# Six slots instead of four through one token tile and then the other around the post-normed sums, and two chunks of the wide layer by rows

## The chip, the cores and the metric

The kernel runs on one core of a Trainium2 chip. Its time is the device time of one execution in microseconds (us). Five engines work side by side and wait for each other through semaphores: PE (TensorE, matmuls), DVE (VectorE), ACT (ScalarE), POOL (GpSimd) and SP, which here only issues the transfers of the weights. Each engine takes its own list of instructions strictly in the order in which it is written: an instruction whose semaphore isn't there yet holds up all that stand behind it on its engine.

## The reference

The program is a small network on 256 tokens of 1024 channels: a state-space layer and an attention layer, and then two blocks of this form (cut to what the change touches):

```
h = rms_norm(x, ln_mix_pre)
merged = g0 * y_mla + g1 * y_conv + g2 * y_ret          # three branches of h, gated
x = x + rms_norm(merged @ w_out, ln_mix_post)           # a post-normed sum
h = rms_norm(x, ln_ffn_pre)
f = (silu(h @ w_gate) * (h @ w_up)) @ w_down            # hidden width 2816
x = x + rms_norm(f, ln_ffn_post)                        # the other post-normed sum
```

All is float32. Each of the two blocks has two post-normed sums, four in all. After three of them the next layer follows (the second norm of block 0, the first norm of block 1, the second norm of block 1); the fourth ends the program.

## The kernel before

**Slots.** The weights are streamed in the order of their use, as slots of 2 x 128 input rows by 512 columns (512 KB; 416 columns in the chunk called lat). A chunk is 512 columns of a weight matrix: `out.` has two chunks of 4 slots, the wide layer `ffn.` 11 chunks of 4 slots (256 gate and 256 up columns side by side), `down.` two chunks of 11 slots. There are six buffers for slots. SP loads a slot as soon as PE is through with the slot six places before it (`sp.wait_ge(slot_used, before[s] + 1)`). To keep float32's precision every operand is split in a high and a low part: ACT writes the high part of a slot's weights (`make_hi`, L1146), DVE the low part (`make_lo`, L1611), and PE multiplies hi x hi, lo x hi and hi x lo (L629 to L631): 6 matmuls of 512 columns for each slot and tile of 128 tokens. I call these six matmuls a tile-slot.

**Order on PE.** `run(n)` takes n slots one after the other, both token tiles of each. `by_tile(n, ...)` takes n slots for token tile 0 and then the same n slots for token tile 1, with steps that are put in before a given tile and slot: `go` transposes four blocks of the next layer's input, `have` waits for their high and low parts. In this way the norm of tile 0 can be worked out while PE is still on tile 1. Buffers of a `by_tile` group come free only in its second half. Chunks of `ffn.` other than the first are computed the other way round (`hidden_slot`, L606 to L608: weights stationary, 12 x 2 matmuls of 256 columns), which gives the hidden layer with its channels on the partitions, as `down.` needs it; the first chunk is computed by rows, since its input isn't there for both tiles at once, and is transposed afterwards (`L{l}.f0`, L1059).

**Order on ACT and DVE.** It is written by hand. `splits(n)` makes the high (ACT) or low (DVE) parts of all slots below n that aren't made yet. `evac` reads a chunk's sums: for `out.` and `down.` ACT squares and adds them (L1180) and DVE multiplies them by the gain into `h_T` (L1644). `post_normed_tail` orders the work behind a post-normed sum for tile 0 and tile 1: `evac`, root on POOL (`root_of_sums`, L2422 and L2407), `residual` (DVE, `x_T`, L1641), `norm_square` (ACT, L1180), a second root on POOL, `apply_norm` (DVE, `h_T`, L1641), the transposes on PE (L684), `tile_hi` (ACT, L1197) and `tile_lo` (DVE, L1641), with `splits` in between.

## Time and profile before

| | us |
|---|---|
| median of 3 runs | 1307.27 (1306.84 to 1309.51) |
| the profiled execution | 1308.64 |
| its span | 1306.8 |
| PE busy | 1248.0 (95%) |
| DVE busy | 920.1 (70%) |
| ACT busy | 633.7 (48%) |
| PE waiting for DVE's `h_T` before the transposes of L684 | 3.7 in 5 waits |
| PE waiting for DVE's `act_F_lo` (L1641) before L629 | 6.5 in 5 waits |

The span is the time between the first and the last record of the profiled execution; some 2 us of its time lie outside. PE is the busy engine nearly everywhere, so time is what PE needs plus what PE waits. Matmuls overlap in the records, so the pace of PE is read from the distance of their starts, not from their durations.

### The profile page before, as it was taken

The numbers are of one execution on the slowest core, as the hardware profiler recorded it, in microseconds if no ns is written. First come the engines' busy times: TensorE is split into PE (matmuls) and PEld (weight loads), VectorE is DVE, ScalarE is ACT, GpSimd is POOL, SyncE is SP. The second block draws the span as 40 slices with busy tenths as digits, with TensorE's granted clock in tenths as the row PEclk, the third lists the DMA queues.
The fourth block names the chain that finished last, engine by engine and source line by source line (L and its number), as shares of the span: only waits on it lengthen the run. The fifth ranks groups of instructions, "written<-read, shape, count | busy, mean of one in ns | idle before, by whom it ended". The sixth has DMA issues, their size and how long they took to land.

```text
span 1306.8 us, 18772 instructions
## 1 busy us (share of the span) xinstructions
PE 1248.0 (95%) x7461; PEld 1039.6 (80%) x7461; DVE 920.1 (70%) x1501; ACT 633.7 (48%) x977; POOL 113.3 (9%) x189
## 2 busy tenths in 40 slices
PE   7799899898999999999999999999999999999998
PEld 3466678787878878777899987888878777999986
DVE  7797778566578997686665554678997686665553
ACT  4334465454555555544544444555555535544442
POOL 7600012000100100201000001100100201000000
PEclk9989999899999999999999999999999999999999
DMA  6734556442664544355656565564444354555553
GB/s 239 210 89 141 181 187 191 130 129 87 193 207 151 157 145 146 121 171 161 193 178 185 186 184 174 186 203 160 146 148 147 125 168 170 167 188 179 183 189 112
DMA packets 71958, 215.73 MB, mean 165 GB/s; under 512 B 16256, under 2 KB 19744, under 8 KB 71744
## 3 DMA queue, kind: packets, MB, share of 16 engines
q1 hardware_dynamic: 65008, 206.43, 49.9%
q0 software_dynamic: 2112, 6.97, 1.7%
q10 hardware_dynamic: 4752, 1.14, 0.4%
q8 instruction: 59, 0.97, 0.3%
q14 instruction: 27, 0.22, 0.1%
HBM read 209.01 MB, written 3.15 MB: 162 GB/s over the span
## 4 chain that ended last, share of the span: by engine, by line
PE 74%; DVE 13%; POOL 4%; ACT 4%; DMA 2%; issue 2%; ACTq 0%; DVEq 0%; POOLq 0%
PE acc L629 16%; PE acc L631 15%; PE acc L630 15%; PE acc L607 6%; PE acc L608 6%; PE acc L606 6%; DVE weights_lo L1611 4%; DVE conv_acc_F L1641 2%; DMA weights_raw<-stream_dram 2%; PE mixed L937 1%; PE acc L569 1%; PE mixed L947 1%; ACT weights_hi L1146 1%; PE mixed L1016 1%; POOL stat L2407 1%
## 5 line engine op out<-in xcount | busy, mean ns | idle before, releaser
L1611 DVE TENSOR_TENSOR weights_lo<-weights_raw,weights_hi 128x1024 fp32r<-128x1024 f32 (+2 forms) x364 | 442.6, 1231 | 230.5 <-ACT weights_hi L1146 229.4
L1146 ACT ACTIVATE weights_hi<-weights_raw 128x1024 fp32r<-128x1024 f32 (+2 forms) x364 | 375.9, 1046 | 293.6 <-DMA weights_raw<-stream_dram 293.4
L629 PE MATMUL acc<-weights_hi,act_F_hi 128*128 128x512 f32 (+1 forms) x896 | 365.0, 407 | 14.0 <-DVE act_F_lo L1641 6.5
L631 PE MATMUL acc<-weights_hi,act_F_lo 128*128 128x512 f32 (+1 forms) x896 | 354.6, 396 | 0.0
L630 PE MATMUL acc<-weights_lo,act_F_hi 128*128 128x512 f32 (+1 forms) x896 | 354.5, 396 | 0.0
L629 PEld LDWEIGHTS acc<-weights_hi,act_F_hi 128*128 128x128 f32 x896 | 170.3, 190 | 54.9 <-DVE act_F_lo L1641 8.0
L631 PEld LDWEIGHTS acc<-weights_hi,act_F_lo 128*128 128x128 f32 x896 | 170.1, 190 | 38.6
L630 PEld LDWEIGHTS acc<-weights_lo,act_F_hi 128*128 128x128 f32 x896 | 170.3, 190 | 35.1
L608 PE MATMUL acc<-act_F_lo,weights_hi 128*128 128x256 f32 x640 | 182.5, 285 | 0.0
L607 PE MATMUL acc<-act_F_hi,weights_lo 128*128 128x256 f32 x640 | 181.9, 284 | 0.0
L606 PE MATMUL acc<-act_F_hi,weights_hi 128*128 128x256 f32 x640 | 180.4, 282 | 0.0
L606 PEld LDWEIGHTS acc<-act_F_hi,weights_hi 128*128 128x128 f32 x640 | 121.8, 190 | 0.1
L608 PEld LDWEIGHTS acc<-act_F_lo,weights_hi 128*128 128x128 f32 x640 | 121.2, 189 | 0.0
L607 PEld LDWEIGHTS acc<-act_F_hi,weights_lo 128*128 128x128 f32 x640 | 120.6, 188 | 0.1
L1641 DVE SCALAR_TENSOR_TENSOR conv_acc_F<-conv_in_F,conv_params,conv_acc_F 128x256 f32<-128x256 f32 x240 | 98.0, 481 | 0.0
L631 PE MATMUL acc<-weights_hi,ffn_F_lo 128*128 128x512 f32 x176 | 69.6, 395 | 0.0
L630 PE MATMUL acc<-weights_lo,ffn_F_hi 128*128 128x512 f32 x176 | 69.6, 395 | 0.0
L629 PE MATMUL acc<-weights_hi,ffn_F_hi 128*128 128x512 f32 x176 | 69.6, 395 | 0.0
L2422 POOL TENSOR_SCALAR stat<-stat 128x1 f32<-128x1 f32 x18 | 9.3, 518 | 638.5 <-ACT junk L1180 638.5
L569 PE MATMUL acc<-weights_raw,hn_F 128*128 128x512 f32 x128 | 58.9, 609 | 0.0
L569 PEld LDWEIGHTS acc<-weights_raw,hn_F 128*128 128x128 f32 x128 | 24.5, 200 | 26.1 <-issue 26.1
L630 PEld LDWEIGHTS acc<-weights_lo,ffn_F_hi 128*128 128x128 f32 x176 | 33.1, 188 | 8.0
(309 smaller groups left out, 1332.4 us busy)
## 6 DMA issues: line engine op xcount, KB each, us to landing
weights_raw<-stream_dram SPq DMA_DIRECT2D x364, 512.0 KB, 3.5
gains<-rows_dram POOLq DMA_DIRECT2D x12, 512.0 KB, 4.8
weights_raw<-stream_dram SPq DMA_DIRECT2D x8, 416.0 KB, 3.2
weights_raw<-stream_dram SPq DMA_DIRECT2D x4, 384.0 KB, 3.0
x_T<-x_in_dram SPq DMA_DIRECT2D x4, 256.0 KB, 6.1
ssm_bc<-ssm_bc_dram SPq DMA_DIRECT2D x1, 1024.0 KB, 8.6
u_scratch<-u_T ACTq DMA_DIRECT2D x4, 256.0 KB, 3.8
u_sub<-u_scratch SPq DMA_DIRECT2D x4, 256.0 KB, 2.8
```

Source lines behind the costliest of these rows:

```text
L569: i = pe.matmul(acc[par][t][:, 0:w], f0[:, k, t * P:(t + 1) * P], raw[:, place[pos], kk * w:(kk + 1) * w], start=first and kk == 0, stop=l ...
L606: pe.matmul(o, wh, hi[:, k, :], start=first and kk == 0 and m % 2 == 0, stop=False, skip_group_check=True)
L607: pe.matmul(o, wl, hi[:, k, :], start=False, stop=False, skip_group_check=True)
L608: i = pe.matmul(o, wh, lo[:, k, :], start=False, stop=last and kk == s["nk"] - 1, skip_group_check=True)
L629: pe.matmul(o, xh, wh, start=first and kk == 0, stop=False)
L630: pe.matmul(o, xh, wl, start=False, stop=False)
L631: i = pe.matmul(o, xl, wh, start=False, stop=last and kk == s["nk"] - 1)
L937: x = pe.matmul(b[:, qt * SEQ:(qt + 1) * SEQ], qk[0:dk, i % 2, qt * P:(qt + 1) * P], qk[0:dk, i % 2, SEQ:2 * SEQ], start=True, stop=True)
L947: x = pe.matmul(b[:, qt * dv:(qt + 1) * dv], probs_t[:, h % 2, qt, kt, :], src_v(kt, h), start=(kt == 0), stop=(kt == TT - 1))
L1146: act.activation(w_hi[:, place[s], 0:n], raw[:, place[s], 0:n], ACT.Copy).then_inc(hi_made, 1)
L1611: dve.tensor_tensor(low(s, slice(0, n)), raw[:, place[s], 0:n], w_hi[:, place[s], 0:n].bitcast(F32), ALU.subtract).then_inc(lo_made, 1)
L1641: return dve.scalar_tensor_tensor(out=o, in0=a, scalar=s, in1=b, op0=op0, op1=op1)
```

## The change

On PE, in each block: the eight slots of `out.` were taken as 2 x `by_tile(4)`, now as `by_tile(2)` and `by_tile(6)`; the first `by_tile(4)` of the wide layer becomes `by_tile(6)` (all of its first chunk and half of the second); the last four slots of `down.` and the four of the next block's `lat.` become groups of six too (in block 1 the last four slots of `down.` stay). The transposes of tile 0's normed input stand before the last slot of tile 1 (`(1, DEEP - 1)`), not behind it. The second chunk of the wide layer is computed by rows and transposed like the first. ACT's and DVE's orders are rewritten for this.

```diff
-FFN_F = HT // 2 - 1
+FFN_T = 2
+FFN_F = HT // 2 - FFN_T
+DEEP = 6
...
             for l in range(DEPTH2):
-                by_tile(4, {(0, 0): [go(0, 0), go(0, 1), have(0, 0)] if l else [have(0, 0)], (0, 2): [have(0, 1)],
-                            (0, 3): [go(1, 0), go(1, 1)], (1, 0): [have(1, 0)], (1, 2): [have(1, 1)]})
-                run(7)
+                n = DEEP if l else 4
+                by_tile(n, {(0, 0): [have(0, 0)], (0, 2): [have(0, 1)],
+                            (0, n - 1): [go(1, 0), go(1, 1)], (1, 0): [have(1, 0)], (1, 2): [have(1, 1)]})
+                run(11 - n)
...
-                by_tile(4, {(0, 0): [have(0, 0)], (0, 2): [have(0, 1), go(1, 1)], (1, 0): [have(1, 0)], (1, 2): [have(1, 1)]})
-                by_tile(4, {})
-                go, have = norm_turner(f"L{l}.h2", 3 + 2 * l)
-                by_tile(4, {(0, 0): [go(0, 0), go(0, 1), have(0, 0)], (0, 2): [have(0, 1)],
-                            (0, 3): [go(1, 0), go(1, 1)], (1, 0): [have(1, 0)], (1, 2): [have(1, 1)]})
-                run(4)
-                pe.wait_ge(ffn0_hid, TT * (l + 1))
-                b = mix(f"L{l}.f0", hid_lo, HT // 2 * l + 1)
+                by_tile(2, {(0, 0): [have(0, 0), have(1, 0), go(1, 1)]})
+                go2, have2 = norm_turner(f"L{l}.h2", 3 + 2 * l)
+                by_tile(DEEP, {(0, 0): [have(0, 1)], (1, 0): [have(1, 1)], (1, DEEP - 1): [go2(0, 0), go2(0, 1)]})
+                by_tile(DEEP, {(0, 0): [have2(0, 0)], (0, 2): [have2(0, 1)],
+                               (0, DEEP - 1): [go2(1, 0), go2(1, 1)], (1, 0): [have2(1, 0)], (1, 2): [have2(1, 1)]})
+                run(4 * FFN_T - DEEP + 3)
+                pe.wait_ge(ffn0_hid, TT * FFN_T * (l + 1))
+                for c in range(FFN_T):
+                    b = mix(f"L{l}.f{c}", hid_lo, HT // 2 * l + c + 1)
...
-                run(HT // 2 - 4)
-                by_tile(4, {})
                 if l + 1 < DEPTH2:
                     go, have = norm_turner(f"L{l + 1}.h", 4 + 2 * l)
+                    run(HT // 2 - DEEP)
+                    by_tile(DEEP, {(1, DEEP - 1): [go(0, 0), go(0, 1)]})
+                else:
+                    run(HT // 2 - 4)
+                    by_tile(4, {})
...
 # ACT, post_normed_tail
-                splits(end + 1)
-                evac(f"L{l}.{kind}1", [0])
-                splits(end + 2)
+                splits(end)
+                for chunk in last:
+                    evac(chunk, [0])
...
-                evac(f"L{l}.{kind}1", [1])
+                splits(end + 1)
                 for half in range(2):
                     tile_hi(name, 0, half, ahead=2)
+                for chunk in last:
+                    evac(chunk, [1])
                 splits(end + 3)
                 for half in range(2):
                     norm_square(name, 1, half, x_normed, x_at + half + 3)
+                splits(end + 5)
                 for half in range(2):
-                    tile_hi(name, 1, half, ahead=4)
+                    tile_hi(name, 1, half, ahead=1)
```

The instructions themselves hardly change; what changes is their order. Three places are shown, in block 0.

On PE, where the gated branches are summed (`gates_T`) and `out.` begins; before the change (rows left out are matmuls of the same kind):

```order
L630 MATMUL acc<-weights_lo,conv_F_hi 128x512
L631 MATMUL acc<-weights_hi,conv_F_lo 128x512
L629 MATMUL acc<-weights_hi,act_F_hi 128x512 [waits conv_weighed,weights_lo_made,turned_lo_made]
L630 MATMUL acc<-weights_lo,act_F_hi 128x512
L631 MATMUL acc<-weights_hi,act_F_lo 128x512
...
L684 MATMUL turned<-consts,gates_T 128x128 [waits merged,turned_lo_made]
L684 MATMUL turned<-consts,gates_T 128x128 x3
```

The same place after the change:

```order
L637 MATMUL acc<-weights_lo,conv_F_hi 128x512
L638 MATMUL acc<-weights_hi,conv_F_lo 128x512
L691 MATMUL turned<-consts,gates_T 128x128 [waits turned_lo_made,merged]
L691 MATMUL turned<-consts,gates_T 128x128 x3
L636 MATMUL acc<-weights_hi,act_F_hi 128x512 [waits conv_weighed,weights_lo_made]
L637 MATMUL acc<-weights_lo,act_F_hi 128x512
```

The last transposes of the summed branches (tile 1, second half) have moved from behind two tile-slots of `out.` to directly behind the matmuls whose sums they need.

On ACT, behind the first post-normed sum (`junk,stat<-acc` is a square of the sums, `junk,stat<-x_T` one of the residual, `weights_hi` a split, `act_F_hi` is `tile_hi`), before the change, from the square of tile 0's last chunk on:

```order
L1180 ACTIVATE junk,stat<-acc 128x512 [waits post_sums,first_tiles_done]
L1146 ACTIVATE weights_hi<-weights_raw 128x1024 [waits weights_in1]
L1180 ACTIVATE junk,stat<-x_T 128x512 [waits post_sums,x_normed]
L1180 ACTIVATE junk,stat<-x_T 128x512 [waits norm_sums,x_normed]
L1180 ACTIVATE junk,stat<-acc 128x512 [waits norm_sums,slots_used]
L1197 ACTIVATE act_F_hi<-turned 128x4x128 [waits turned_ready] x2
L1146 ACTIVATE weights_hi<-weights_raw 128x1024 [waits weights_in2]
...
L1146 ACTIVATE weights_hi<-weights_raw 128x1024 [waits weights_in3]
```

After the change, from the split of the wide layer's first slot (`weights_in0`) on:

```order
L1158 ACTIVATE weights_hi<-weights_raw 128x1024 [waits weights_in0]
L1209 ACTIVATE act_F_hi<-turned 128x4x128 [waits turned_ready] x2
L1192 ACTIVATE junk,stat<-acc 128x512 [waits norm_sums,slots_used]
L1192 ACTIVATE junk,stat<-acc 128x512 [waits post_sums,slots_used]
L1158 ACTIVATE weights_hi<-weights_raw 128x1024 [waits weights_in1]
L1158 ACTIVATE weights_hi<-weights_raw 128x1024 [waits weights_in2]
L1192 ACTIVATE junk,stat<-x_T 128x512 [waits post_sums,x_normed]
L1192 ACTIVATE junk,stat<-x_T 128x512 [waits norm_sums,x_normed]
L1158 ACTIVATE weights_hi<-weights_raw 128x1024 [waits weights_in3]
L1158 ACTIVATE weights_hi<-weights_raw 128x1024 [waits weights_in4]
L1209 ACTIVATE act_F_hi<-turned 128x4x128 [waits turned_ready] x2
L1158 ACTIVATE weights_hi<-weights_raw 128x1024 [waits weights_in5]
```

The splits of the second and later slots of the next group now stand behind the squares of tile 1 (`slots_used`); before, the first two were done ahead of them.

On DVE at the same place (`h_T<-acc,gains` is `evac`, `x_T` the residual, `h_T<-x_T` the norm, `act_F_lo` is `tile_lo`, `weights_lo` a split), before the change, from tile 0's norm on:

```order
L1641 SCALAR_TENSOR_TENSOR h_T<-x_T,stat,gains 128x512
L1611 TENSOR_TENSOR weights_lo<-weights_raw,weights_hi 128x1024 [waits weights_hi_made]
L1644 TENSOR_TENSOR h_T<-acc,gains 128x512 [waits gain_in0,post_sums,slots_used]
L1641 SCALAR_TENSOR_TENSOR act_F_lo<-turned,act_F_hi 128x4x128 [waits turned_hi_made]
L1641 SCALAR_TENSOR_TENSOR x_T<-h_T,stat,x_T 128x512 [waits post_roots,mix_scaled]
```

After the change, likewise:

```order
L1656 SCALAR_TENSOR_TENSOR h_T<-x_T,stat,gains 128x512
L1626 TENSOR_TENSOR weights_lo<-weights_raw,weights_hi 128x1024 [waits weights_hi_made]
L1656 SCALAR_TENSOR_TENSOR act_F_lo<-turned,act_F_hi 128x4x128 [waits turned_hi_made] x2
L1659 TENSOR_TENSOR h_T<-acc,gains 128x512 [waits gain_in0,post_sums,slots_used] x2
L1626 TENSOR_TENSOR weights_lo<-weights_raw,weights_hi 128x1024 [waits weights_hi_made] x2
L1656 SCALAR_TENSOR_TENSOR x_T<-h_T,stat,x_T 128x512 [waits post_roots,mix_scaled]
L1656 SCALAR_TENSOR_TENSOR x_T<-h_T,stat,x_T 128x512
L1626 TENSOR_TENSOR weights_lo<-weights_raw,weights_hi 128x1024 [waits weights_hi_made]
```

Both low parts of tile 0 now stand ahead of tile 1's `evac`; of the six slots of the next group one is split ahead of it, two behind it, and one behind the residual (then come the norm of tile 1, one more split, `tile_lo` twice, and the sixth split).

## Rows read from the trace of the kernel before

**Rows 1.** The page's first part: busy us (share of the span), instructions.

```profile
PE 1248.0 (95%) x7461; PEld 1039.6 (80%) x7461; DVE 920.1 (70%) x1501; ACT 633.7 (48%) x977; POOL 113.3 (9%) x189
```

**Rows 2.** Waits of PE over the span: us in total, times, longest.

```profile
PE acc L629 <- DVE act_F_lo L1641: 6.5, 5, 1.6
...
PE acc L629 <- DVE weights_lo L1611: 3.4, 8, 1.4
```

**Rows 3.** Timeline of PE, begin of block 0's `out.`: start, us, instruction.

```profile
594.47 0.39 PE L629 MATMUL acc<-weights_hi,act_F_hi 128*128 128x512 f32 x1
...
597.25 0.60 PE L684 MATMUL turned<-consts,gates_T 128*128 128x128 f32 x4
597.60 0.48 PE L629 MATMUL acc<-weights_hi,act_F_hi 128*128 128x512 f32 x1
```

**Rows 4.** Timeline of PE, end of block 0's `out.` and on.

```profile
617.73 0.40 PE L631 MATMUL acc<-weights_hi,act_F_lo 128*128 128x512 f32 x1
618.86 1.29 PE L684 MATMUL turned<-consts,h_T 128*128 128x128 f32 x8 [0.74 <-DVE h_T L1641]
621.77 0.50 PE L629 MATMUL acc<-weights_hi,act_F_hi 128*128 128x512 f32 x1 [1.61 <-DVE act_F_lo L1641]
...
623.61 0.63 PE L629 MATMUL acc<-weights_hi,act_F_hi 128*128 128x512 f32 x1
624.04 0.63 PE L630 MATMUL acc<-weights_lo,act_F_hi 128*128 128x512 f32 x1
...
635.46 0.28 PE L606 MATMUL acc<-act_F_hi,weights_hi 128*128 128x256 f32 x1
...
646.86 0.60 PE L1059 MATMUL mixed<-consts,ffn_hid_F 128*128 128x128 f32 x4
```

**Rows 5.** Timeline of PE, end of block 0's `down.` and the next block's `lat.`.

```profile
812.35 0.40 PE L631 MATMUL acc<-weights_hi,ffn_F_lo 128*128 128x512 f32 x1
...
816.80 0.35 PE L629 MATMUL acc<-weights_hi,act_F_hi 128*128 128x416 f32 x1
816.99 0.35 PE L630 MATMUL acc<-weights_lo,act_F_hi 128*128 128x416 f32 x1
...
827.67 0.40 PE L629 MATMUL acc<-weights_hi,act_F_hi 128*128 128x512 f32 x1
```

**Rows 6.** Timeline of PE, block 1: begin of `out.` and end of `ffn.0`.

```profile
1083.34 0.39 PE L629 MATMUL acc<-weights_hi,act_F_hi 128*128 128x512 f32 x1
...
1123.77 0.28 PE L606 MATMUL acc<-act_F_hi,weights_hi 128*128 128x256 f32 x1
```

**Rows 7.** Timeline of ACT, end of block 0's `out.`.

```profile
612.58 0.60 ACT L1180 ACTIVATE junk<-acc 128x512 f32<-128x512 f32 x1 [0.72 <-PE acc L631]
...
613.17 1.05 ACT L1146 ACTIVATE weights_hi<-weights_raw 128x1024 fp32r<-128x1024 f32 x1
...
618.16 0.60 ACT L1180 ACTIVATE junk<-acc 128x512 f32<-128x512 f32 x1 [1.38 <-PE acc L631]
...
619.53 1.26 ACT L1197 ACTIVATE act_F_hi<-turned 128x512 fp32r<-128x512 f32 x2 [0.68 <-PE turned L684]
```

**Rows 8.** Timeline of DVE, end of block 0's `out.`.

```profile
613.36 0.69 DVE L1644 TENSOR_TENSOR h_T<-acc,gains 128x512 f32<-128x512 f32 x1 [0.20 <-issue]
...
614.46 1.41 DVE L1641 SCALAR_TENSOR_TENSOR x_T<-h_T,stat,x_T 128x512 f32<-128x512 f32 x2 [0.40 <-POOL stat L2407]
...
617.97 1.42 DVE L1641 SCALAR_TENSOR_TENSOR h_T<-x_T,stat,gains 128x512 f32<-128x512 f32 x2 [2.10 <-POOL stat L2407]
...
619.30 1.22 DVE L1611 TENSOR_TENSOR weights_lo<-weights_raw,weights_hi 128x1024 fp32r<-128x1024 f32 x1
```

**Rows 9.** Timeline of POOL, end of block 0's `out.`.

```profile
616.88 0.30 POOL L2422 TENSOR_SCALAR stat<-stat 128x1 f32<-128x1 f32 x1 [2.54 <-ACT junk L1180]
...
618.95 1.66 POOL L2422 TENSOR_SCALAR stat<-stat 128x1 f32<-128x1 f32 x1 [1.11 <-ACT junk L1180]
```

**Rows 10.** Source view of the slots' loads (L1127), 590 to 640 us.

```profile
DMA to landing us min/median/max: 3.2/4.7/5.4
```

**Rows 11.** Timeline of DVE, begin of block 0's `out.`: the last sum of the gated branches.

```profile
595.47 0.69 DVE L1644 TENSOR_TENSOR gates_T<-gates_T 128x512 f32<-128x512 f32 x1
```

117 lines of the change are left out of this document (64 added, 53 removed).

## The prediction

> **What bounds the kernel now.** I read the page's busy shares first, then the waits of PE, and then the timeline of PE, ACT, DVE and POOL around the post-normed sums, each at the same stretch. PE is busy 95% of the span, DVE 70% [rows 1], and of its waits those for `act_F_lo` and for `weights_lo` matter here [rows 2]. So the time is PE's work at the full clock (2.4 GHz) plus what PE waits, and a change of order can only move waits. The reader is to see three things.
>
> First, PE's pace. Twelve matmuls of 512 columns start between 594.47 and 597.25, where the transposes come [rows 3]: 0.232 us each, 1.39 us for a tile-slot of six. A slot of the wide layer in the other form takes (646.86 - 635.46) / 4 = 2.85 us [rows 4] against 2.78 for two tile-slots. A tile-slot of lat has starts 0.19 apart [rows 5]: 1.14.
>
> Second, what a post-normed sum costs now. PE is through with tile 1 of `out.` at 617.96 (617.73 and one pace) and starts the wide layer at 621.77; between them lie 0.8 us of transposes and 3.0 of waiting. From 621.77 to 635.46 it does 48 matmuls and eight transposes, 11.9 us of work, in 13.7: starts stand 0.43 apart for a while, not 0.23 [rows 4], the lower clock level of 1.2 GHz behind a stretch of waiting. The loss is 4.8 us (3.0 and 1.8). Block 1 does the same work from the start of `out.` on in 40.4 us, block 0 in 41.0 [rows 3, 4, 6], so I take the same loss there. At the end of `down.`, from 812.58 to 827.67, PE does 8 tile-slots of lat and 16 transposes (10.7) in 15.1, a loss of 4.4 [rows 5]. The three together are 14.0 us: all that the change can take away.
>
> Third, the chain of tile 0 behind its last matmul: from the square at 612.58 to the transposes at 618.86 it is 6.3 us, over DVE, POOL, DVE, ACT, POOL, DVE [rows 4, 7 to 9]. Tile 1 of four slots covers 5.56 us, tile 1 of six covers 8.34.
>
> **The change, part by part.** I reckon from T, the moment when PE is through with the last tile-slot before the norm, and number the slots of `out.` 0 to 7, those of the next layer 8 to 13.
>
> *Tile 0's chain is covered.* With the transposes before the last slot, PE reaches them 5 x 1.39 = 6.95 us after tile 0's end; the first half of the norm is there after 6.5, the second 0.7 later, and the four transposes of the first half lie between. `tile_hi` follows 0.67 after its transposes and `tile_lo` 0.6 later [rows 4, 7], within the last slot's 1.39. The 3.0 us of waiting are gone at each place. What is late next is the weights.
>
> *The new group's weights.* All six buffers belong to the group that PE is working on, and the next group's slots can be split only as tile 1 frees them. The order lets one of the six be split before tile 1's sums, the rest behind. From T, with the durations of the rows:
> - Slot 8 is ready, PE works on it until T+1.4. ACT's square of tile 1 starts at T+0.2 (617.96 to 618.16), the high part of slot 9 takes T+0.8 to T+1.85 [rows 7]; DVE's `evac` starts 0.78 behind the square and lasts 0.6, the low part takes 1.22 [rows 8]: done at T+3.1. PE waits **1.8**.
> - DVE splits slot 10 (T+4.3) and then does the residual, whose first half is there at T+4.9; only then come ACT's two squares (T+5.0, 0.8 apart), and behind them the high part of slot 11 (T+6.4 to T+7.5) and its low part (to T+8.75). PE wanted it at T+5.95: **2.8**.
> - DVE does tile 1's norm from T+8.65 (the root on POOL is there at T+7.6, one microsecond behind the sums [rows 9]) to T+10.0, then the low part of slot 12 to T+11.2. PE wanted it at T+10.15: **1.1**.
> - After slot 12 PE transposes tile 1 (T+12.6 to T+13.4). Slot 13 is split behind both `tile_hi` and both `tile_lo`: T+13.3, two of them 1.0, the high part to T+15.35, the low part from T+15.4 to T+16.6. PE wanted it at T+13.4: **3.2**.
>
> The sum is 8.9 us. Slot loads take 3.2 to 5.4 us from issue to landing [rows 10]; slots 9 to 12 were freed between T-6.4 and T-2.2 and slot 13 at T, and would have landed before the point at which the order reaches them, so the transfers are not what PE waits for here. The last slot of a six-group is freed only five tile-slots (6.95) before its use: 0.3 + 4.7 + 1.05 + 1.2 = 7.25, another **0.3** in `out.`.
>
> *The merge.* PE passes the last transposes of `gates_T` directly behind the matmuls of which they are made. At 594.47 PE goes on to `out.` today; DVE's last sum ends at 596.16 [rows 3, 11]. PE will wait **1.75** us there, twice, and everything on PE is behind it. Today 12 matmuls cover it.
>
> *Sum for `out.`,* from PE's start on it to the end of slot 13: 1.75 + 0.35 (four transposes) + 16 tile-slots of 22.25 + 0.8 + 0.3 = 25.4 to T; then 16.6, a tile-slot of 1.4, and tile 1 of six, 8.3: 51.8 us. Today the same slots take 635.46 - 594.47 + 2 x 2.85 = 46.7 in block 0 and 1123.77 - 1083.34 + 5.7 = 46.1 in block 1 [rows 3, 4, 6]. **+5.1 and +5.7.**
>
> *Sum for `down.`:* the same steps with lat's shorter tile-slots and splits (832 columns for 1024) give waits of 1.7, 2.8, 1.3 and 3.2; slot 13 begins at T+15.75. From the start of the six slots (812.58 - 16.7 = 795.9) it is 16.7 + 0.8 + 15.75 + 1.4 + 4 x 1.14 + 2.8 = 42.0; today to 827.67 and two slots of 2.78 more, 37.3 [rows 5]. **+4.6.**
>
> *The second chunk by rows.* Two more slots in the cheaper form per block, -0.15; four more transposes with the restart behind them, 0.35 + 0.1; two `ffn_F_lo` now stand on DVE ahead of the next weight split, some 0.2. Per block +0.5, in all **+1.0**; its bounds are -0.3 (hidden altogether) and +2.
>
> *The clock.* No row shows PE with this pattern of waits. Below, it is nothing: a half-speed matmul that lies in front of a wait costs nothing, since DVE sets the pace there. Above, two stretches at the lower level per place, 1.8 us each by the loss found above. I take one per place, like two of today's three: 3 x 1.8 = **+5.4**, and keep 0 and 10.8 as ends. The Trainium skill (TensorE: Matmul & The Clock Gate, section "HAM oscillation — how this bites in real kernels") says that short work between long waits falls back to the low clock again and again, and reckons the penalty as half of the time spent there; by that rule it would be the upper end, 5 us more than my sum. This trace agrees in so far as the starts of rows 4 are 0.43 apart after a wait, and disagrees at `down.`, where the starts stay 0.19 apart.
>
> POOL's first operation of a root took 0.30 us once and 1.66 when DVE was splitting weights beside it [rows 8, 9]. With more splits beside the roots tile 1's norm can come up to 0.4 us later at each place; I leave that in the range. The Trainium skill (SBUF — State Buffer, section "Who interferes with whom") has the rule behind it: the two engines share a pair of ports that one holds for a whole instruction.
>
> Total: 5.1 + 5.7 + 4.6 + 1.0 + 5.4 = **+21.8 us**. The profiled execution took 1308.64 us (span 1306.8 and some 2 us outside); it becomes 1330.4. It stands 1.4 above the median of the runs, 1307.27, so I forecast 1329.
>
> **The rivals.**
> *The cover works and nothing takes its place (faster).* The mechanism is the ring of six buffers: it decides whether slots 9 to 13 are split by the time PE wants them. If they were, as slots 8 to 11 are today, PE would get back 4.8 + 4.8 + 4.4 and pay 2 x 1.75 at the merge and 1.0 for the chunk: -9.5, 1298. The point is 1.39 us behind T: slot 9's low part there or not. For it speaks that DVE is idle 30% of the time; against it that ACT has the split written behind a square that can't start before T. 6 in 100.
> *No change.* The waits of one or two of the six steps are half of mine (shorter handovers, `evac` earlier) and the clock stays up: this needs 15 us of error in a chain whose terms are read one by one. 2 in 100. With part of that, a time of 1310 to 1319: 7 in 100.
> *The clock falls twice and more at each place.* 16.4 + 10.8 and the late roots: +28, 1335 or above. The broken work in the 15 us behind T speaks for it, only five of them are PE's; against it `down.` today. 12 in 100.
> *Transfers.* Six slots in one go could land ever later. At 1.39 us between frees they landed after 4.7, at most 5.4 [rows 10]; each us beyond 5.4 would add at most 1 at slot 9 and nothing at the others. Inside my range.
>
> **How the numbers follow.** Forecast as worked out (1320 to 1335): 73 in 100, the others as above. Slower in all is 92, faster 6, no change 2 (within 0.2%, 2.6 us, about what a measurement of this kernel can tell). The range leaves the faster case and the smallest of the slower ones out and goes from 1316 to 1338.
>
> **What would show it.** In the timeline of PE after the change: the transposes of `h_T` without a wait before them; four waits for `weights_lo` in the first half of each six-slot group, before its second, fourth, fifth and sixth slot, the last the longest (3 us); a wait of 1.7 before the last transposes of `gates_T`, twice. PE's waits for `weights_lo` should sum to 25 to 30 us (3.4 today over the whole kernel [rows 2]), those for `act_F_lo` shrink. ACT's split of slot 9 should start within a microsecond behind the square of tile 1. If PE doesn't wait for `weights_lo` there, the prediction is wrong in its main step; if the waits are there but the sum of time is smaller, the clock term is.

## The result, and the profile after

| | before | after |
|---|---|---|
| median of 4 runs each, us | 1307.05 (1304.73 to 1309.51) | 1333.23 (1331.00 to 1334.67) |
| ratio, 95% interval | | 1.0209 (1.0183 to 1.0235) |
| profiled execution, span | 1308.64, 1306.8 | 1331.00, 1328.8 |
| granted clock over the span | 0.990 | 0.986 (the four runs: 0.983 to 0.986) |

The change makes the kernel 2.1% slower, 26 us. I forecast 1329 with a range of 1316 to 1338. The spans of the two profiled executions differ by 22.0 us; the medians by 4 more, since the profiled execution of the kernel after is the fastest of its four and that of the kernel before lies 1.6 us above its median.

The page's first part, of the kernel after (it answers to [rows 1]):

```profile
PE 1249.8 (94%) x7373; PEld 1034.8 (78%) x7373; DVE 920.2 (69%) x1505; ACT 632.9 (48%) x979; POOL 110.0 (8%) x189
```

PE has 1.8 us more busy time, DVE and ACT have the same to within 1 us: what the change adds is waiting. PE's waits over the span, of the kernel after (us in total, times, longest; [rows 2] before):

```profile
PE acc L636 <- DVE weights_lo L1626: 27.8, 18, 2.9
...
PE turned L691 <- DVE gates_T L1659: 4.0, 4, 1.7
...
PE turned L691 <- DVE h_T L1656: 1.5, 2, 1.2
PE acc L636 <- DVE act_F_lo L1656: 1.5, 1, 1.5
```

The waits for split weights went from 3.4 to 27.8 us; those for `act_F_lo` fell from 6.5 to 1.5, and those for `h_T` from 3.7 to 1.5 (the rest lies elsewhere). Tile 0's chain is covered, as the change wants, and another wait has taken its place. Where it stands shows the timeline of PE in block 0, of the kernel after:

```profile
592.55 0.40 PE L638 MATMUL acc<-weights_hi,conv_F_lo 128*128 128x512 f32 x1
594.63 0.63 PE L691 MATMUL turned<-consts,gates_T 128*128 128x128 f32 x4 [1.68 <-DVE gates_T L1659]
...
616.25 1.03 PE L691 MATMUL turned<-consts,h_T 128*128 128x128 f32 x8
...
618.29 0.39 PE L638 MATMUL acc<-weights_hi,act_F_lo 128*128 128x512 f32 x1
...
621.66 0.50 PE L636 MATMUL acc<-weights_hi,act_F_hi 128*128 128x512 f32 x1 [1.58 <-DVE weights_lo L1626]
...
627.24 0.50 PE L636 MATMUL acc<-weights_hi,act_F_hi 128*128 128x512 f32 x1 [2.51 <-DVE weights_lo L1626]
...
629.70 0.50 PE L636 MATMUL acc<-weights_hi,act_F_hi 128*128 128x512 f32 x1 [0.79 <-DVE weights_lo L1626]
...
635.19 0.50 PE L636 MATMUL acc<-weights_hi,act_F_hi 128*128 128x512 f32 x1 [2.94 <-DVE weights_lo L1626]
...
636.09 0.63 PE L636 MATMUL acc<-weights_hi,act_F_hi 128*128 128x512 f32 x1
636.51 0.63 PE L637 MATMUL acc<-weights_lo,act_F_hi 128*128 128x512 f32 x1
...
652.19 0.28 PE L613 MATMUL acc<-act_F_hi,weights_hi 128*128 128x256 f32 x1
```

The eight transposes at 616.25 have no wait (they had 0.74, and 1.61 behind them [rows 4]). The last matmul of `out.` starts at 618.29, so PE is through with it at 618.52, one pace later. The four waits behind are the second, fourth, fifth and sixth slot of the wide layer. From 636.09 the starts stand 0.43 apart, the lower clock level. Who made PE wait is seen on ACT and DVE, first ACT, of the kernel after, same stretch:

```profile
618.72 0.60 ACT L1192 ACTIVATE junk<-acc 128x512 f32<-128x512 f32 x1 [0.17 <-PE acc L638]
...
623.44 0.63 ACT L1192 ACTIVATE junk<-x_T 128x512 f32<-128x512 f32 x1 [2.15 <-DVE x_T L1656]
...
624.89 1.99 ACT L1158 ACTIVATE weights_hi<-weights_raw 128x1024 fp32r<-128x1024 f32 x2
631.85 1.08 ACT L1209 ACTIVATE act_F_hi<-turned 128x512 fp32r<-128x512 f32 x2 [4.97 <-PE turned L691]
632.82 1.06 ACT L1158 ACTIVATE weights_hi<-weights_raw 128x1024 fp32r<-128x1024 f32 x1
```

And DVE, of the kernel after:

```profile
622.66 1.41 DVE L1656 SCALAR_TENSOR_TENSOR x_T<-h_T,stat,x_T 128x512 f32<-128x512 f32 x2
625.96 1.23 DVE L1626 TENSOR_TENSOR weights_lo<-weights_raw,weights_hi 128x1024 fp32r<-128x1024 f32 x1 [1.89 <-ACT weights_hi L1158]
...
632.48 1.29 DVE L1656 SCALAR_TENSOR_TENSOR act_F_lo<-turned,act_F_hi 128x512 fp32r<-128x512 f32 x2 [2.83 <-ACT act_F_hi L1209]
633.91 1.22 DVE L1626 TENSOR_TENSOR weights_lo<-weights_raw,weights_hi 128x1024 fp32r<-128x1024 f32 x1
```

PE, ACT and DVE wait for each other in turn. ACT stands idle for 2.15 us in front of the residual's squares (623.44) although the fourth slot's split is written behind them, and DVE then idles 1.89 for that split (625.96). Both idle (4.97 and 2.83 us) in front of tile 1's parts, although the sixth slot's split stands behind them. No row of the stretch ends on a transfer.

In block 1's `out.` the waits are 1.61, 2.54, none and 2.94. At `down.` and lat the same four waits as in block 0 appear (1.48, 2.47, 0.98 and 2.89), and two things more. PE, of the kernel after, from the fifth slot on:

```profile
828.29 0.79 PE L636 MATMUL acc<-weights_hi,act_F_hi 128*128 128x512 f32 x1 [0.98 <-DVE weights_lo L1626]
831.01 1.91 PE L691 MATMUL turned<-consts,h_T 128*128 128x128 f32 x8
835.81 0.80 PE L636 MATMUL acc<-weights_hi,act_F_hi 128*128 128x512 f32 x1 [2.89 <-DVE weights_lo L1626]
...
854.96 0.50 PE L636 MATMUL acc<-weights_hi,act_F_hi 128*128 128x512 f32 x1 [2.38 <-DVE weights_lo L1626]
```

First, the clock. A view of stretches, of the kernel after (from 827.2 to 840.9 us; us, then busy time and count of PE, PEld, DVE, ACT, POOL; granted clock, share of the transfers, GB/s):

```profile
827.20:840.90 13.70, 9.83 (x29) 7.95 (x29) 3.78 (x6) 2.14 (x3) 0.53 (x1) 0.51 0.25 81
```

13.7 us at a granted clock of 0.51, that is the lower of the two levels (1.2 GHz); the slot and the eight transposes from 828.29 on take twice their time (1.91 us for the transposes against 1.03 at 616.25). Second, a wait of 2.38 us 19 us later, which the kernel before doesn't have. On ACT, of the kernel after:

```profile
844.29 1.06 ACT L1158 ACTIVATE weights_hi<-weights_raw 128x1024 fp32r<-128x1024 f32 x1 [9.79 <-DMA weights_raw<-stream_dram]
846.82 1.06 ACT L1158 ACTIVATE weights_hi<-weights_raw 128x1024 fp32r<-128x1024 f32 x1 [1.47 <-DMA weights_raw<-stream_dram]
847.79 0.50 ACT L1243 ACTIVATE lat_T<-acc 128x416 f32<-128x416 f32 x1
```

The reading of lat's sums, and the norm behind them (on DVE at 852.37, after 3.23 us of waiting for POOL's root), stand behind the splits of two slots whose transfers could start only when the group's second half freed their buffers.

**The sum.** Milestones on PE, from the timelines of the two kernels (`out.` counted from the end of conv_o.; "slot 15" is the end of the wide layer's second chunk). The rows not yet shown, first of the kernel before:

```profile
750.98 0.40 PE L629 MATMUL acc<-weights_hi,ffn_F_hi 128*128 128x512 f32 x1
847.19 0.27 PE L724 MATMUL turned<-consts,lat_norm_T 128*128 128x128 f32 x1
1135.16 0.27 PE L1059 MATMUL mixed<-consts,ffn_hid_F 128*128 128x128 f32 x1
1239.29 0.40 PE L629 MATMUL acc<-weights_hi,ffn_F_hi 128*128 128x512 f32 x1
```

Then of the kernel after:

```profile
755.82 0.39 PE L636 MATMUL acc<-weights_hi,ffn_F_hi 128*128 128x512 f32 x1
817.79 0.40 PE L638 MATMUL acc<-weights_hi,ffn_F_lo 128*128 128x512 f32 x1
843.86 0.35 PE L638 MATMUL acc<-weights_hi,act_F_lo 128*128 128x416 f32 x1
863.44 0.27 PE L731 MATMUL turned<-consts,lat_norm_T 128*128 128x128 f32 x1
1101.48 0.63 PE L691 MATMUL turned<-consts,gates_T 128*128 128x128 f32 x4 [1.68 <-DVE gates_T L1659]
1157.94 0.28 PE L613 MATMUL acc<-act_F_hi,weights_hi 128*128 128x256 f32 x1
1261.56 0.39 PE L636 MATMUL acc<-weights_hi,ffn_F_hi 128*128 128x512 f32 x1
```

| stretch | before | after | difference | forecast |
|---|---|---|---|---|
| start to `out.`, block 0 (same code) | 594.47 | 592.78 | -1.7 | 0 |
| `out.` to slot 15 | 52.39 | 59.41 | +7.0 | 5.1 + 1.8 |
| wide layer to `down.` | 104.12 | 103.63 | -0.5 | +0.5 |
| `down.` to sixth slot of block 1 | 82.2 | 91.0 | +8.8 | 4.6 + 1.8 |
| to the transposes of lat | 14.0 | 16.6 | +2.6 | 0 |
| to `out.`, block 1 | 236.15 | 236.2 | 0 | 0 |
| `out.` to slot 15 | 51.82 | 58.3 | +6.5 | 5.7 + 1.8 |
| wide layer to `down.` | 104.13 | 103.62 | -0.5 | +0.5 |
| `down.` to the end | 67.5 | 67.2 | -0.3 | 0 |
| sum | 1306.8 | 1328.8 | +22.0 | +21.8 |

(592.78 is 592.55 and one pace; 1099.63, the end of conv_o. in block 1, is the transposes' 1101.48 less block 0's distance of 1.85; the sixth slot ends two tile-slots of 1.39 behind 843.86 + 0.19, and before the change two slots of 2.78 behind 827.67. The -0.5 of the wide layer, twice, is a difference in the pace of its matmuls and not what the second chunk costs; see x_rows below.)

### The profile page after: what moved, and what is told of

Same layout as the page of the kernel before. It is cut to its first block, busy times and chain, and to the rows that moved or that the text cites. A ratio compares the mean times of both kernels' runs of the same rounds, so it can differ in the third digit from the quotient of the medians.

```text
span 1328.8 us, 18602 instructions
## 1 busy us (share of the span) xinstructions
PE 1249.8 (94%) x7373; PEld 1034.8 (78%) x7373; DVE 920.2 (69%) x1505; ACT 632.9 (48%) x979; POOL 110.0 (8%) x189
## 4 chain that ended last, share of the span: by engine, by line
PE 72%; DVE 14%; ACT 5%; POOL 4%; DMA 2%; issue 2%; ACTq 0%; DVEq 0%; POOLq 0%
PE acc L636 15%; PE acc L638 15%; PE acc L637 15%; PE acc L613 5%; PE acc L615 5%; PE acc L614 5%; DVE weights_lo L1626 5%; DVE conv_acc_F L1656 2%; DMA weights_raw<-stream_dram 2%; ACT weights_hi L1158 2%; PE mixed L944 1%; PE acc L576 1%; PE mixed L954 1%; POOL stat L2434 1%; PE mixed L1024 1%
## 5 line engine op out<-in xcount | busy, mean ns | idle before, releaser
L636 PE MATMUL acc<-weights_hi,act_F_hi 128*128 128x512 f32 (+1 forms) x928 | 379.5, 409 | 33.0 <-DVE weights_lo L1626 27.8
L638 PE MATMUL acc<-weights_hi,act_F_lo 128*128 128x512 f32 (+1 forms) x928 | 368.2, 397 | 0.0
L637 PE MATMUL acc<-weights_lo,act_F_hi 128*128 128x512 f32 (+1 forms) x928 | 367.9, 396 | 0.0
L613 PE MATMUL acc<-act_F_hi,weights_hi 128*128 128x256 f32 x576 | 162.6, 282 | 0.0
L615 PE MATMUL acc<-act_F_lo,weights_hi 128*128 128x256 f32 x576 | 162.2, 282 | 0.0
L614 PE MATMUL acc<-act_F_hi,weights_lo 128*128 128x256 f32 x576 | 162.1, 281 | 0.0
L613 PEld LDWEIGHTS acc<-act_F_hi,weights_hi 128*128 128x128 f32 x576 | 108.4, 188 | 0.2
L614 PEld LDWEIGHTS acc<-act_F_hi,weights_lo 128*128 128x128 f32 x576 | 108.5, 188 | 0.1
L615 PEld LDWEIGHTS acc<-act_F_lo,weights_hi 128*128 128x128 f32 x576 | 108.4, 188 | 0.0
L1209 ACT ACTIVATE act_F_hi<-turned 128x512 fp32r<-128x512 f32 x32 | 18.4, 596 | 46.5 <-PE turned L691 46.3
```

Of the source, the lines that this page charges most:

```text
L613: pe.matmul(o, wh, hi[:, k, :], start=first and kk == 0 and m % 2 == 0, stop=False, skip_group_check=True)
L614: pe.matmul(o, wl, hi[:, k, :], start=False, stop=False, skip_group_check=True)
L615: i = pe.matmul(o, wh, lo[:, k, :], start=False, stop=last and kk == s["nk"] - 1, skip_group_check=True)
L636: pe.matmul(o, xh, wh, start=first and kk == 0, stop=False)
L637: pe.matmul(o, xh, wl, start=False, stop=False)
L638: i = pe.matmul(o, xl, wh, start=False, stop=last and kk == s["nk"] - 1)
```

## The experiments

All ratios are to the kernel before, run beside each kernel on the same chip; "us" is the median. The kernel before has medians of 1305.2 to 1307.1 us in the different experiments, so a difference between kernels of two experiments carries that much uncertainty beside the intervals. Below "second slot" and so on are slots of the new group, T the end of the group before, on PE.

| kernel | base and edit | us | ratio (95%) | clock, mean |
|---|---|---|---|---|
| x_last | after, sixth slot split ahead of tile 1's parts | 1320.5 | 1.0101 (1.0087 to 1.0115) | 0.989 |
| x_merge | after, transposes of `gates_T` later | 1325.1 | 1.0145 (1.0124 to 1.0167) | 0.987 |
| v_merge | before, transposes of `gates_T` early | 1310.7 | 1.0038 (1.0024 to 1.0052) | 0.991 |
| x_rows | before, second chunk by rows | 1305.1 | 0.9993 (0.9984 to 1.0003) | 0.992 |
| x_down | before, groups of six at `down.` only | 1314.3 | 1.0062 (1.0047 to 1.0076) | 0.990 |
| y_nine | x_last, second slot ahead of tile 1's squares | 1318.9 | 1.0089 (1.0060 to 1.0117) | 0.988 |
| y_eleven | x_last, fourth slot ahead of the residual's squares | 1316.7 | 1.0081 (1.0053 to 1.0108) | 0.990 |
| y_six | all four orders | 1311.2 | 1.0038 (1.0023 to 1.0053) | 0.991 |
| y_five | the same, groups of five | 1307.5 | 1.0007 (0.9994 to 1.0020) | 0.994 |
| w_six | y_six, `evac` and lat earlier | 1306.7 | 1.0002 (0.9991 to 1.0014) | 0.991 |
| w_five | y_five, the same, and `out.` as 2, 1, 5 | 1304.8 | 0.9986 (0.9977 to 0.9996) | 0.994 |
| v_pool | w_five, three low parts on POOL | 1308.1 | 1.0011 (0.9998 to 1.0024) | 0.990 (0.994 without one run at 0.944) |

(The before kernel's runs have a mean granted clock of 0.992, those of the kernel after 0.984.)

### x_last: the sixth slot ahead of tile 1's parts

```diff
 # ACT, and the same on DVE before tile_lo
-                splits(end + 5)
+                splits(end + 6)
                 for half in range(2):
                     tile_hi(name, 1, half, ahead=1)
```

> The kernel after, with the sixth slot's high and low parts written ahead of tile 1's `tile_hi` and `tile_lo` (ACT and DVE: `splits(end + 6)` for `splits(end + 5)`). Theory of the order: the 2.9 us that PE waits before the sixth slot at each of three places come only from the split standing behind both parts of tile 1; DVE stands idle for 4.5 us in front of them. The wait goes, and about 0.7 us comes back as a wait for `act_F_lo` one tile-slot later: 3 x -2.2 = -6.6 us, 1326 to 1328. Rival, the ring: the sixth slot's buffer is freed last, its weights have not landed any earlier and the wait stays at 2.5 us or more: 0 to -1 us.

Measured: 1320.5, about 13 us less than the kernel after (expected: 1326 to 1328). The wait is gone at all three places, and no other comes in its place. On DVE, of x_last, block 0, the last two low parts now stand together and it idles afterwards:

```profile
629.02 2.35 DVE L1626 TENSOR_TENSOR weights_lo<-weights_raw,weights_hi 128x1024 fp32r<-128x1024 f32 x2
634.74 0.69 DVE L1656 SCALAR_TENSOR_TENSOR act_F_lo<-turned,act_F_hi 128x512 fp32r<-128x512 f32 x1 [3.36 <-ACT act_F_hi L1209]
```

The theory of the order stands, the ring's doesn't: ACT makes three high parts in a row from 625.48 on (2.94 us, no wait for a transfer among them), the sixth slot's among them, so the buffer freed last was filled by 627.4, about 3 us before PE began the fifth slot (630.29). The gain is twice what I expected. The 0.7 us that should have come back did not (tile 1's parts are made while PE is on the sixth slot), which makes 3 x 2.9 = 8.8; the spans differ by 9.7. The rest of the medians' difference goes with the clock, 0.989 for 0.984.

### x_merge and v_merge: the merge, undone and done alone

```diff
 # x_merge, on the kernel after
-                by_tile(2, {(0, 0): [have(0, 0), have(1, 0), go(1, 1)]})
+                by_tile(2, {(0, 0): [have(0, 0)], (1, 0): [have(1, 0), go(1, 1)]})
 # v_merge, on the kernel before
-                by_tile(4, {(0, 0): [have(0, 0)], (0, 2): [have(0, 1), go(1, 1)], (1, 0): [have(1, 0)], (1, 2): [have(1, 1)]})
+                by_tile(4, {(0, 0): [have(0, 0), have(1, 0), go(1, 1)], (0, 2): [have(0, 1)], (1, 2): [have(1, 1)]})
```

> The kernel after, with the last transposes of `gates_T` behind two tile-slots of `out.`, as before the change. Theory of the merge: the waits of 1.68 us go at both places and nothing takes their place, since tile 1's second half is first wanted six tile-slots later: -3.4 us, about 1329.8. Rival: the start of `out.` only moves to an earlier time and PE meets the same chain of splits a little later; the waits for split weights before the second to sixth slot of the wide layer stand at a fixed distance from the end of `out.`, so this would need a wait inside `out.`; then 0 to -1 us.

> The kernel before with one edit: the last transposes of `gates_T` stand directly behind the matmuls whose sums they need, as in the change; everything else is as before. Prices the merge term from the other side: my prediction has 1.75 us at two places, +3.5. Undoing the same edit in the kernel after (x_merge) gave back 8 us in the medians. If that surplus belongs to the clock, which falls more often where several waits lie within 30 us, then here, with only one other wait of 2.4 us near, it stays at +3 to +4.5: 1309.5 to 1311, granted clock unchanged at 0.99. If the two waits themselves cost more than their length, it is +7 or more here too.

Measured: x_merge is 8 us faster than the kernel after, v_merge 5.0 us slower than the kernel before (interval 3.1 to 6.8). In both traces the wait of 1.68 us stands or goes at both places, with nothing in its place. v_merge is between its two cases, nearer to the first, and its interval holds the 3.4 us of the two waits themselves. In the kernel after, undoing the merge gave back 8 us in the medians; with both intervals that is some 4 to 13, and the spans of the profiled executions differ by 5.8. That the merge costs more there than alone is likely but not shown. If so, the surplus goes with the clock: in x_merge's profiled execution no stretch at `down.` is at the lower level as long as the 13.7 us above. That the waits themselves call the lower level up isn't shown.

### x_rows: the second chunk alone

```diff
 # kernel before; the wide layer's code as in the change, DEEP left at four
-FFN_F = HT // 2 - 1
+FFN_T = 2
+FFN_F = HT // 2 - FFN_T
```

> The kernel before, with only the second chunk of the wide layer by rows (groups of four slots everywhere). My prediction's term for it: +1.0 us in all (bounds -0.3 and +2). The trace of the kernel after, from the end of slot 15 to the start of `down.`, has 0.5 us less per block, not more: then -1.0 us against the kernel before. Rival: two chunks wanted at once from ACT and DVE hold up the splits behind them, +3 us or more.

Measured: 0.9993, -0.9 us, between -2.1 and +0.4, close to the -1.0 read from the kernel after. The forecast's +1.0 lies outside; no wait appears behind the two chunks. But the traces show that the -1.0 in the spans isn't what the chunk costs. The 256-column matmuls of a block start either 0.1199 or 0.1187 us apart, on the mean of some 860 of them, and that alone makes 1.0 to 1.2 us per block. In the profiled kernel before both blocks have the slower pace, in the profiled kernel after both the faster. v_merge has the kernel before's code there and the faster pace in block 0:

```profile
648.83 0.60 PE L1059 MATMUL mixed<-consts,ffn_hid_F 128*128 128x128 f32 x4
...
751.80 0.39 PE L629 MATMUL acc<-weights_hi,ffn_F_hi 128*128 128x512 f32 x1
```

| wide layer to `down.`, us | pace 0.1199 | pace 0.1187 |
|---|---|---|
| one chunk by rows | 104.1 (4 blocks: both of before, block 1 of x_down and v_merge) | 103.0 (block 0 of x_down and v_merge) |
| two chunks by rows | 104.6 (2 blocks: of x_merge and w_five) | 103.5 to 103.6 (the other 20 blocks) |

At the same pace the second chunk costs 0.4 to 0.7 us per block, as forecast. Why a block has one pace or the other, and whether it is chance that the slower one stands in four of six blocks of the old form and in two of 22 of the new, the runs don't show.

### x_down: groups of six at one place

```diff
 # kernel before; n = DEEP if l else 4 at the start of a block, six last slots of down. by tile,
 # and the change's ACT and DVE order for this place alone
+                (tail_of_six if kind == "down." and name else tail_of_four)(name, l, kind, no)
```

> The kernel before, with groups of six only at the end of block 0's `down.` and the start of block 1's `lat.`, one place of three. If the places are independent: the forecast's terms for it are 4.6 + 1.8 = +6.4 us; the trace of the kernel after has +11.4 there (8.8 in the groups, 2.6 in a wait behind `lat.`). I expect +9 to +12, with the wait of 2.4 us behind `lat.` there too. Rival: the wait behind `lat.` and the long stretch at the lower clock come from the kernel's other changes and not from this place; then +6 or less.

Measured: +8.1 us (6.1 to 9.9), less than the 9 to 12 that I expected. Waits of 1.49, 2.47, 1.05 and 2.94 in the group and of 1.84 behind lat stand in its trace. The place does by itself what it does in the whole change, a little less: its stretch at the lower level is shorter (820.5 to 829.9) and its wait behind lat too. The time alone would hardly exclude the rival's +6; the rows do, since both the wait and the stretch are there without the other changes.

### y_nine and y_eleven: which waits only move

```diff
 # y_nine, on x_last; the same on DVE
+                splits(end + 2)
                 for chunk in last:
                     evac(chunk, [1])
 # y_eleven, on x_last, ACT alone
-                splits(end + 3)
+                splits(end + 4)
                 for half in range(2):
                     norm_square(name, 1, half, x_normed, x_at + half + 3)
```

> The kernel x_last with the second slot of the new group split ahead of tile 1's squares (ACT) and of tile 1's `evac` (DVE). The prediction priced the wait before that slot as a term of its own. If the waits add up, the 1.5 us before the second slot go at three places: -4.5 us against x_last, 1316. Rival theory, DVE's list: behind T DVE has the same splits, residual and norm to do, in whatever order, so the 1.2 us come back before the fourth slot (its wait grows from 2.5 to over 3) and the time stays within 1 us of x_last's 1320.5; I hold this for likelier, since the square of tile 1, and with it the residual, now waits for that split.

> The kernel x_last with the fourth slot's high part ahead of the two squares of tile 1's residual on ACT (`splits(end + 4)` for `splits(end + 3)`), DVE as it is. In the trace of the kernel after ACT stands idle 1.9 us before those squares, and DVE 1.7 us before the fourth slot's low part. Theory of the order: the wait before the fourth slot falls from 2.5 to about 0.9 us, and the norm of tile 1 comes 0.5 us earlier: 3 x -1.6 to -2 = -5 to -6 us, 1315. Rival, the transfer: the slot has landed only a little before ACT reaches it, so it can't be split earlier: within 1 us of 1320.5.

Measured: y_nine 1318.9 (1.6 below x_last), y_eleven 1316.7 (3.8 below, for 5 to 6 expected). By the intervals of the ratios neither time differs from x_last's for certain; the waits in the rows decide. PE of y_nine, block 0:

```profile
623.24 0.47 PE L636 MATMUL acc<-weights_hi,act_F_hi 128*128 128x512 f32 x1 [0.76 <-DVE weights_lo L1627]
627.59 0.50 PE L636 MATMUL acc<-weights_hi,act_F_hi 128*128 128x512 f32 x1 [2.70 <-DVE weights_lo L1627]
630.05 0.80 PE L636 MATMUL acc<-weights_hi,act_F_hi 128*128 128x512 f32 x1 [0.66 <-DVE weights_lo L1627]
```

And of y_eleven:

```profile
622.12 0.50 PE L636 MATMUL acc<-weights_hi,act_F_hi 128*128 128x512 f32 x1 [1.58 <-DVE weights_lo L1626]
625.72 0.50 PE L636 MATMUL acc<-weights_hi,act_F_hi 128*128 128x512 f32 x1 [0.56 <-DVE weights_lo L1626]
629.22 0.50 PE L636 MATMUL acc<-weights_hi,act_F_hi 128*128 128x512 f32 x1 [1.83 <-DVE weights_lo L1626]
```

x_last waits 1.61, 2.52 and 0.58 there. In y_nine the first wait is down to 0.17, and 1.0 us of it is back (0.76 before the third slot, 0.18 more before the fourth, 0.08 before the fifth): DVE's theory is mostly right. In y_eleven the fourth slot's wait fell by 2.0 and the fifth's grew by 1.25, behind tile 1's norm, which now is late: a part I hadn't foreseen. Here only removed idle time of DVE counted; a slot put ahead of another piece of work hands the wait on.

### y_six and y_five: all orders together, and groups of five

```diff
 # y_six: x_merge, x_last, y_nine and y_eleven in one
 # y_five, on y_six (out. as three and five slots; cut to the main lines)
-DEEP = 6
+DEEP = 5
-                by_tile(2, {(0, 0): [have(0, 0)], (1, 0): [have(1, 0), go(1, 1)]})
+                by_tile(3, {(0, 0): [have(0, 0)], (0, 2): [have(0, 1), go(1, 1)], (1, 0): [have(1, 0)], (1, 2): [have(1, 1)]})
 # ACT and DVE
-                splits(end)
+                splits(end + 1)
```

> The kernel after with all four changes of order together: gates_T's last transposes behind two tile-slots, and the second, fourth and sixth slot split ahead of tile 1's squares, of the residual's squares and of tile 1's parts. If what DVE has to do behind T is the limit (five splits of 1.22, `evac` 0.6, residual and norm 1.4 each, two parts 1.3: 10.8 us beside 9.1 us of PE), each place still waits 1.7 to 2.5 us, against 7.8 in the kernel after: -16 and -3.4 for the merge, and up to -5 of clock: 1309 to 1313, no faster than before. If the waits of the kernel after are all a matter of order, they go: 1302 to 1305.

> The same order with groups of five slots, and the first slot of the next group split ahead of everything. By DVE's work behind T: four splits, 9.6 us beside 7.75 us of PE and a chain of 6.5 us that must fit into four tile-slots (5.6): about 1 us of wait before the transposes of tile 0 and again of tile 1, 1 us for the weights: 3 per place, as much as before the change, 1306 to 1310. If the ring is what counts (one buffer more that is free at T), it is faster than y_six by 3 us or more: 1303 to 1306.

Measured: 1311.2 and 1307.5. y_six is as the theory of DVE's load expects in time; its waits are longer than the 1.7 to 2.5 us expected: PE waits 0.16, 0.76, 0.73 and 1.84 before the second to fifth slot at both places of `out.`. That is 3.5 us instead of 7.8. y_five lies in the range of the first theory (1306 to 1310), with some 3 us of waits per place as it says, but is also 3.7 us faster than y_six, which was the sign of the other. So y_five doesn't decide between DVE's load and the ring: it has one split less behind T and one buffer more free at T, both at once. About 21 of the 26 us that the change cost were thus order, merge and the clock that went with them, not groups of six as such. But y_six is still 5 us slower than before.

### w_six and w_five: two more moves

```diff
 # ACT; DVE likewise between tile 0's norm and its parts
+                for chunk in last[:-1]:
+                    evac(chunk, [1])
                 for half in range(2):
                     tile_hi(name, 0, half, ahead=2)
 ...
             for l in range(DEPTH2):
-                run(8)
+                evac(f"L{l}.lat.0", [0])
+                splits(pos + (DEEP + 1 if l else 6))
+                evac(f"L{l}.lat.0", [1])
+                pos += 4
+                run(4)
 # w_five only, on PE
-                by_tile(3, {(0, 0): [have(0, 0)], (0, 2): [have(0, 1), go(1, 1)], (1, 0): [have(1, 0)], (1, 2): [have(1, 1)]})
+                by_tile(2, {(0, 0): [have(0, 0)], (1, 0): [have(1, 0), go(1, 1)]})
+                have(0, 1)()
+                have(1, 1)()
+                run(1)
```

> The kernel y_six with two more moves. `evac` of out.0 for tile 1 stands behind tile 0's norm, not behind T (0.6 us of DVE and 0.8 of ACT less behind T, at the two places of `out.`); and in both blocks the sums of lat. are read as soon as PE is through with them, ahead of the split of slot 15. If DVE's work behind T is the limit, the waits of 0.76, 0.73 and 1.84 at those places shrink by about 0.6 in sum, the wait of 2.7 behind `lat.` by 2 or more: -3.5 us against y_six's 1311.2, 1307 to 1309. If the chain of tile 1 or the transfers are the limit there, only the part behind `lat.` shows: -2.

> The kernel y_five with the same two moves, and `out.` taken as two slots by tile, one slot for both tiles, and then five by tile, so that the ring's buffers come free earlier before the group (y_five waits 0.5 and 1.2 us inside `out.` for its last slots). Waits at `out.` 3.1 to 2.0 each, behind `lat.` 1.3 to 0.3: -3 us against y_five's 1307.5: 1304 to 1305.5, a ratio of 0.998 to 1.000 to the kernel before. A faster version than 1303 would mean that the clock stays up everywhere as well.

Measured: 1306.7 and 1304.8, w_six a bit better than expected. Its waits at block 0's `out.` are 0.16, 0.75 and 1.83, 0.7 less in sum than y_six's, so DVE's load did count there. The wait behind lat is gone in both (2.71 in y_six, 1.28 in y_five), so it was what the ACT rows at 844.29 say. w_five is the only version with groups deeper than four that beats the kernel before, by 0.14% (0.04 to 0.23%). Its waits in block 0, on PE, are 0.73 before the transposes of `h_T`, and 0.73 and 0.42 for split weights: 1.9 us against 2.4 in the kernel before. The clock goes with it, at 0.994 in w_five's runs for 0.992.

### v_pool: a low part on POOL

```diff
 # POOL, between its two roots of tile 1; DVE leaves this slot out, PE waits for its own semaphore
+                            pool.wait_ge(hi_made, s + 1 - WHOLE)
+                            pool.tensor_tensor(low(s, slice(0, n)), raw[:, place[s], 0:n], w_hi[:, place[s], 0:n].bitcast(F32),
+                                               ALU.subtract).then_inc(pool_lo, 1)
```

> The kernel w_five with one low part of the next group, that of its third slot, made by POOL instead of DVE at each of the three places (between POOL's two roots of tile 1). It tests whether DVE's list behind T is what the tuned kernels still wait for. From the rows of the kernel before, 2048 columns took POOL 4.6 us, so 1024 should take 2.3 (DVE: 1.22); the split then ends 2.4 us behind ACT's high part, 0.9 us later than PE wants it, but residual and norm of tile 1 come 1.1 us earlier and the waits before the fourth and fifth slot (0.73 and 0.42) go. If DVE's list is the limit: -0.3 to -1 us per place, 1302 to 1304. Rival, the two engines hold each other up: POOL's 2.3 us become 3.5 or more and DVE's residual beside it slows down from 1.4 to 2.5: then slower than w_five, 1306 or more.

Measured: 1308.1, 3 us slower than w_five: the rival's time, and one half of its mechanism. DVE and then POOL, of v_pool, block 0:

```profile
619.58 3.43 DVE L1672 SCALAR_TENSOR_TENSOR x_T<-h_T,stat,x_T 128x512 f32<-128x512 f32 x2 [0.32 <-POOL stat L2452]
```

```profile
619.43 2.36 POOL L2592 TENSOR_TENSOR weights_lo<-weights_raw,weights_hi 128x1024 fp32r<-128x1024 f32 x1
```

POOL's part takes the 2.36 us that I expected, but DVE's residual beside it takes 3.43 us, not 1.42. PE waits 1.57 us for POOL, where I had 0.9, and 0.63 and 0.42 for DVE behind it. The kernel before had shown the same at another place:

```profile
451.65 4.59 POOL L2407 TENSOR_TENSOR ret_g_T<-ret_g_T,gains 128x2048 f32<-128x2048 f32 x1 [105.36 <-DVE ret_g_T L1641]
452.15 6.32 DVE L1611 TENSOR_TENSOR weights_lo<-weights_raw,weights_hi 128x1024 fp32r<-128x1024 f32 x2
```

The first row is where my 4.6 us came from. Beside it two splits of DVE took 6.32 us, not 2.4: I had read POOL's price there and not DVE's.

## Why the prediction was right

**What bounds the kernel.** PE's waits decide, and its busy time hardly moved: right.

**Tile 0's chain is covered.** Right at all three places: no wait before the transposes of `h_T`, none for `act_F_lo` behind them.

**The new group's weights.** Right, step by step. T is 618.52 in block 0 (ACT's square starts 0.2 behind it, as I had it). I had the second slot at T+3.1, the fourth at T+8.75, the fifth at T+11.2 and the sixth at T+16.6; the rows have T+3.1, T+8.7, T+11.2 and T+16.7. The waits are 1.58, 2.51, 0.79 and 2.94 for my 1.8, 2.8, 1.1 and 3.2. The constant difference of some 0.25 is one of reading: a wait in brackets is counted from the modelled end of the last matmul, mine from start plus one pace. PE's waits for `weights_lo` sum to 27.8 us, for 25 to 30 forecast. The 0.3 us before the last slot of the six in `out.` didn't come: its matmuls start 0.36 apart at 607.77 instead of 0.23, with no wait. The experiments say which were real causes: the sixth (x_last) and the fourth (y_eleven) came from an order that let ACT and DVE idle; the second is mostly DVE's load (y_nine). My sentence on the transfers also holds there. It doesn't hold 10 us later, behind lat.

**The merge.** 1.75 forecast, 1.68 in brackets and 1.85 between starts. As a term of time, 3.5 us forecast, 5.0 (3.1 to 6.8) alone (v_merge) and about 8 (4 to 13) in the kernel after (x_merge): perhaps too small.

**Sum for `out.`** +7.0 and +6.5 with the clock, for 6.9 and 7.5.

**Sum for `down.`** With the clock too small: +8.8 for 6.4, and 2.6 more behind lat. Two steps failed. The first is in the clock's term. "A half-speed matmul that lies in front of a wait costs nothing, since DVE sets the pace there": at 828.29 the clock was down for the fifth slot and for tile 1's transposes, and the sixth slot's split hangs on these transposes through `tile_hi` and `tile_lo`. From the fifth slot's start to the transposes it took 2.72 us for 1.51 in block 0, from there to the sixth slot 4.80 for 3.98. So the sixth slot began at T+17.8 (T is 818.02), not T+15.75. The rest of the stretch cost 2.2 us more, behind the waits, so the clock cost 4.2 us at this place for my 1.8; without it the sum of 4.6 stands. The other step is that I stopped at the group's end: the next wait stands behind lat's norm.

**The second chunk by rows.** As a time it has the wrong sign: +1.0 forecast, -1.0 in the spans, -0.9 (-2.1 to +0.4) alone. As the cost of the added steps it is right: at the same pace of the 256-column matmuls they cost 0.4 to 0.7 us per block. What I hadn't seen is that this pace has two values, worth 1.0 us and more per block, and that the profiled kernel before had the slower one in both.

**The clock.** I took 5.4, three times 1.8, of 0 to 10.8. In the profiled execution one stretch at each place is down: 636.1 to 639.5, 827.2 to 840.9 and 1134.4 to 1137.8. The first, behind the last wait, cost 1.6 us (nine steps between starts took 3.64 us, 2.09 at full pace); the second 4.2, as above. The third covers the fourth slot, before which PE had waited 2.54 us, and part of the fifth, which then has no wait; the sixth begins at T+17.2 (T is 1125.24), where block 0 has T+16.7. So it cost 0.5: there my sentence on half-speed matmuls in front of a wait held for the most part. The sum is 6.3 for 5.4, with the places far apart. Over the runs the mean granted clock is 0.984, in the profiled one 0.986; a stretch at the lower level lowers the mean by half its share of the span and loses at most half its length, so an ordinary run of the kernel after pays up to 3 us more.

**The total.** +22.0 between the spans for a forecast of +21.8 is partly luck: `down.` and lat cost 5.0 more than I said, against -2.0 for the wide layer, which comes from the pace (at one pace for both kernels the spans would differ by some 24), -0.9 for `out.`, -0.3 at the end, and -1.7 from the start of the program, where the code is the same.

**The rivals.** "The cover works and nothing takes its place" named the right point (the second slot's low part) and the wrong owner: I gave it to the ring of six buffers. y_nine has it there (a wait of 0.17 is left) and x_last and y_eleven have the sixth and the fourth slot: the lists of ACT and DVE held these slots, not their buffers. Whether the ring has a part where groups of five do better than six (3.7 us, y_five and y_six) is open, since DVE's load behind T changes there too. More buffers weren't tried.

## What to carry to other kernels

When a group is made deeper to cover one chain, write down what the helper engines have to do from the group's end to its next use, and check each of them for idle time in front of an item whose follower is ready: such idle time is what a new order gave back here; the rest of a wait mostly moved. A strictly ordered list should hold the work that is ready ahead of the work that waits for the engine it feeds. Follow the change one norm further than the place that it touches, since late splits are late for the next reader too. And before a small difference between two traces is put down to the change, compare the pace of the same instructions in both: here 1% of pace over 100 us outweighed the term in question.
